# State-space heads of a two-layer diffusion backbone: one exponential and a predicated copy per head instead of masks and eight exponentials

## The reference

```python
seg = cum[:, :, :, None] - cum[:, :, None]
lmat = jnp.exp(jnp.where(causal, seg, -jnp.inf))
cb = jnp.einsum('bctgn,bcsgn->bctsg', cc, bc)
y_diag = jnp.einsum('bctsgh,bcsghp->bctghp', cb[..., None] * lmat, xdt)
...
y = (y_f + y_b + d_skip[:, None] * xs).reshape(bsz, m, SSM_D_INNER) * jax.nn.silu(z)
```

## Time and profile before

| | us |
|---|---|
| median of 3 runs | 2121.7 |
| lowest and highest | 2121.1, 2123.09 |
| the profiled execution's own time | 2116.36 |
| its span in the profile | 2114.6 |
| TensorE busy | 2039.2 |
| VectorE busy | 1275.2 |
| ScalarE busy | 863.0 |
| GpSimd busy | 114.3 |

### The profile page before, as it was taken

How to read it: one execution, slowest core, us unless ns; L and a number is a source line. 1 busy time by engine, 2 the same in 40 slices (tenths; PEclk the granted TensorE clock), 3 DMA queues, 4 the chain that set the end, 5 groups by cost and what they waited for, 6 DMA issues and landing times.

```text
span 2114.6 us, 33441 instructions
## 1 busy us (share of the span) xinstructions
PE 2039.2 (96%) x12674; PEld 1802.4 (85%) x12674; DVE 1275.2 (60%) x1958; ACT 863.0 (41%) x1392; POOL 114.3 (5%) x175
## 2 busy tenths in 40 slices
PE   6999999999999999999999999999998999999998
PEld 4899999998889999999998877778775787888887
DVE  7655655557475773764766767777777644333335
ACT  4544433434232341332433555748384325222222
POOL 1111001010010000000000100000000000000000
PEclk9999999999999999999999999999999999999999
DMA  8422232323422432433322221221216223333332
GB/s 311 140 81 83 68 90 81 91 61 120 119 87 78 138 116 80 138 96 96 98 88 66 77 70 41 66 64 50 89 48 230 64 86 86 93 99 97 93 99 90
DMA packets 297916, 204.68 MB, mean 97 GB/s; under 512 B 5396, under 2 KB 289421, under 8 KB 296013
## 3 DMA queue, kind: packets, MB, share of 16 engines
q1 hardware_dynamic: 294349, 180.04, 29.0%
q0 software_dynamic: 3456, 23.09, 3.0%
HBM read 189.47 MB, written 13.63 MB: 96 GB/s over the span
## 4 chain that ended last, share of the span: by engine, by line
PE 81%; DVE 8%; ACT 5%; issue 3%; DMA 1%; SPq 1%; ACTq 0%; POOL 0%; DVEq 0%; POOLq 0%
PE G L328 56%; PE G L1241 13%; ACT e L1995 1%; PE S L2133 1%; PE S L874 1%; DVE acc L2164 1%; PE S L2129 1%; PE S L845 1%; PE S L453 1%; DVE wlo L315 1%; DVE hlo L755 1%; DVE hn L746 1%; ACT whi L311 1%; PE G L437 1%; DMA ada<-in_ada_w_dram 1%
## 5 line engine op out<-in xcount | busy, mean ns | idle before, releaser
L328 PE MATMUL G<-hhi,whi 128*128 128x384 f32 (+2 forms) x1760 | 573.9, 377 | 25.5 <-DVE hlo L755 16.2
L315 DVE TENSOR_TENSOR wlo<-raw,whi 128x1024 fp32r<-128x1024 f32 (+2 forms) x213 | 248.0, 1165 | 471.9 <-ACT whi L311 471.3
L328 PE MATMUL G<-hhi,wlo 128*128 128x384 f32 (+2 forms) x1760 | 531.4, 352 | 0.0
L328 PE MATMUL G<-hlo,whi 128*128 128x384 f32 (+2 forms) x1760 | 531.0, 352 | 0.0
L311 ACT ACTIVATE whi<-raw 128x1024 fp32r<-128x1024 f32 (+2 forms) x213 | 215.9, 1014 | 718.6 <-PE G L328 584.5
L328 PEld LDWEIGHTS G<-hhi,whi 128*128 128x128 f32 x1760 | 318.8, 190 | 92.0 <-issue 39.6
L328 PEld LDWEIGHTS G<-hhi,wlo 128*128 128x128 f32 x1760 | 326.5, 190 | 20.1
L328 PEld LDWEIGHTS G<-hlo,whi 128*128 128x128 f32 x1760 | 327.1, 190 | 17.7
L328 PE MATMUL G<-mhi,whi 128*128 128x384 f32 (+2 forms) x544 | 163.6, 349 | 2.0 <-issue 0.9
L328 PE MATMUL G<-mhi,wlo 128*128 128x384 f32 (+2 forms) x544 | 162.6, 347 | 0.0
L328 PE MATMUL G<-mlo,whi 128*128 128x384 f32 (+2 forms) x544 | 162.5, 347 | 0.0
(11 more groups left out here) (356 smaller groups left out, 2991.6 us busy)
## 6 DMA issues: line engine op xcount, KB each, us to landing
raw<-in_ffn_w_in_dram SPq DMA_DIRECT2D x52, 512.0 KB, 4.0
raw<-in_ssm_w_in_dram SPq DMA_DIRECT2D x41, 512.0 KB, 4.0
raw<-in_hg_w_in_dram SPq DMA_DIRECT2D x40, 512.0 KB, 4.1
adaw<-in_ada_w_dram SPq DMA_DIRECT2D x20, 1024.0 KB, 5.3
adaf<-in_ada_w_dram SPq DMA_DIRECT2D x20, 1024.0 KB, 5.3
sraw<-in_ffn_w_in_dram SPq DMA_DIRECT2D x36, 512.0 KB, 5.1
raw<-in_ffn_w_out_dram SPq DMA_DIRECT2D x32, 384.0 KB, 3.6
raw<-in_ssm_w_out_dram SPq DMA_DIRECT2D x16, 512.0 KB, 4.1
```

What stands on the lines that cost most here:

```text
L315: dve.tensor_tensor(wlo[pn.slot][:, 0:kt, :], raw[pn.slot][:, 0:kt, :], f32(whi[pn.slot][:, 0:kt, :]), ALU.subtract).then_inc(s["lo"], 1)
L328: ins = pe.matmul(G[:, tl.slot, g0:g0 + n], w[pn.slot][:, k, :], r[:, k_base + k, t0:t0 + n], start=(first and k == 0 and i == 0), stop=(l ...
```

## The change

Per head TensorE issues one matmul for each direction. The selector `hsel` now has 48 rows, and `hrow` beside it holds the cuts of this group, so that the product already contains the shift that was ScalarE's bias. The masks are gone. The earlier direction is in bank 0, the later one in bank 1 for even and bank 3 for odd heads. ScalarE copies bank 0 to the tile `e` (`head_start`), VectorE overwrites the later direction's half from the other bank with a predicated copy under the constant mask `later` (`head_select`), and ScalarE takes one exponential of 128x512 in place (`head_decays`). VectorE multiplies by `cb`. Every output goes to bank 2, so that `heads_y` of hh waits for `head_out` of hh - 1.

A predicated copy gives each pair of tokens one direction, so a token's product with itself is counted once. The other one and the skip are computed on GpSimd (`own_tokens`) and added to `ytm` ahead of the heads' outputs, and `yb` is written by one multiplication with z. GpSimd also fetches the rows of each group from DRAM (`head_rows`).

```diff
-            def pair_decays(hh):
-                r = hh % 2
+            def head_start(hh):
                 act.wait_ge(s["sm"], HPG * q + hh + 1)
                 if hh >= 2:
                     act.wait_ge(s["yd"], HPG * q + hh - 1)
-                for d in (0, 1):
-                    for b in range(LBLK):
-                        ins = act.activation(block(m[f"e{d}{r}"][:, :], b), block(S[:, d, :], b), ACT.Exp,
-                                             bias=m["shiftT"][:, b, bass.ds(q * HPG + (d * NH + hh), 1)])
-                ins.then_inc(s["em"], 1)
+                act.activation(m[f"e{hh % 2}"][:, :], S[:, 0, :], ACT.Copy).then_inc(s["ec"], 1)
+            def head_decays(hh):
+                act.wait_ge(s["sl"], HPG * q + hh + 1)
+                e = m[f"e{hh % 2}"][:, :]
+                act.activation(e, e, ACT.Exp).then_inc(s["em"], 1)
...
                         if q is not None and 3 <= j < 7:
-                            pair_decays(2 * (j - 3))
-                        if q is not None and ci == 1:
-                            act.wait_ge(s["skip"], q * GT + GT)
+                            head_start(2 * (j - 3))
                         if ci:
                             convolved(ci - 1)
+                        if q is not None and 3 <= j < 7:
+                            head_decays(2 * (j - 3))
...
-                if q is not None and j == 1:
-                    act.wait_ge(s["yout"], q * 32 + 16)
-                    for i_ in range(GT):
-                        act.activation(m["yb"][:, i_, :], m["xfm"][:, i_, 0:NLAT], ACT.Identity,
-                                       scale=m["dsk"][:, bass.ds(q * GT + i_, 1)]).then_inc(s["skip"], 1)
                 if q is not None and 3 <= j < 7:
                     if before is None:
-                        pair_decays(2 * (j - 3))
-                    pair_decays(2 * (j - 3) + 1)
+                        head_start(2 * (j - 3))
+                        head_decays(2 * (j - 3))
+                    head_start(2 * (j - 3) + 1)
+                    head_decays(2 * (j - 3) + 1)
...
+        def later_bank(hh):
+            return 3 if hh % 2 else 1
+        def head_select(dve, q, hh):
+            dve.wait_ge(s["ec"], HPG * q + hh + 1)
+            dve.memset(m["carry"][:, :], 0.0)
+            dve.copy_predicated(by_block(m[f"e{hh % 2}"][:, :]), m["later"][:, :, :].to_broadcast([P, LBLK, P]),
+                                by_block(S[:, later_bank(hh), :])).then_inc(s["sl"], 1)
         def head_weights(dve, q, hh):
-            r = hh % 2
             dve.wait_ge(s["em"], HPG * q + hh + 1)
-            e0, e1 = m[f"e0{r}"][:, :], m[f"e1{r}"][:, :]
-            dve.tensor_tensor(e0, e0, e1, ALU.add).then_inc(s["mm"], 1)
-            dve.wait_ge(s["mm"], 2 * (HPG * q + hh) + 1)
-            dve.tensor_tensor(e0, e0, m["cb"][:, :], ALU.mult).then_inc(s["mm"], 1)
+            e = m[f"e{hh % 2}"][:, :]
+            dve.tensor_tensor(e, e, m["cb"][:, :], ALU.mult).then_inc(s["mm"], 1)
         def head_out(dve, q, hh):
+            if hh == 0:
+                dve.wait_ge(s["owna"], 2 * q + 2)
             dve.wait_ge(s["yd"], HPG * q + hh + 1)
             yt = m["ytm"][:, :, hh * HP:(hh + 1) * HP]
-            dve.tensor_tensor(yt, yt, S[:, 2 + hh % 2, 0:LBLK * HP].rearrange("p (b c) -> p b c", c=HP),
+            dve.tensor_tensor(yt, yt, S[:, 2, 0:LBLK * HP].rearrange("p (b c) -> p b c", c=HP),
                               ALU.add).then_inc(s["ym2"], 1)
...
+                h0 = 2 * (j - 3)
                 if q is not None and 3 <= j < 7:
-                    head_weights(dve, q, 2 * (j - 3))
                     if j > 3:
-                        head_out(dve, q, 2 * (j - 3) - 1)
+                        head_out(dve, q, h0 - 2)
+                    head_select(dve, q, h0)
+                    head_weights(dve, q, h0)
+                    if j > 3:
+                        head_out(dve, q, h0 - 1)
                 for u in range(4):
                     if q is not None and j < 3:
                         chain_vector(dve, q, 4 * j + u)
+                    if q is not None and 3 <= j < 7 and u == 3:
+                        head_select(dve, q, h0 + 1)
                     tap(u + 1)
                 if q is None:
                     for _ in range(DT_DVE.count(j)):
                         next(dt)
                 if q is not None and 3 <= j < 7:
-                    head_weights(dve, q, 2 * (j - 3) + 1)
-                    head_out(dve, q, 2 * (j - 3))
+                    head_weights(dve, q, h0 + 1)
                 if q is not None and j == 7:
                     if ss is None:
                         split_lo(dve, At(PAN_SO + SO_SPLITS[j]), KT)
+                    head_out(dve, q, HPG - 2)
                     head_out(dve, q, HPG - 1)
                     for i_ in range(GT):
                         yb = m["yb"][:, i_, :]
                         dve.wait_ge(s["ytt"], GT * q + i_ + 1)
-                        dve.tensor_tensor(yb, yb, S[:, i_, :], ALU.add).then_inc(s["ya"], 1)
-                    for i_ in range(GT):
-                        yb = m["yb"][:, i_, :]
-                        dve.wait_ge(s["ya"], GT * q + i_ + 1)
-                        dve.tensor_tensor(yb, yb, m["z"][:, bass.ds(q % 2, 1), i_, :].rearrange("p a t -> p (a t)"),
+                        dve.tensor_tensor(yb, S[:, i_, :], m["z"][:, bass.ds(q % 2, 1), i_, :].rearrange("p a t -> p (a t)"),
                                           ALU.mult).then_inc(s["yz"], 1)
...
+        def head_rows(pool, g):
+            hs = slice(g * HPG, (g + 1) * HPG)
+            for e in (0, 1):
+                for d in (0, 1):
+                    r = (2 * e + d) * HPG
+                    pool.dma_start(m["hrow"][r:r + HPG, :], cut_park[e, d, hs, :]).then_inc(s["hin"], 16)
+                    pool.dma_start(m["hsel"][HK + e * LBLK:HK + (e + 1) * LBLK, d * HPG:(d + 1) * HPG, :],
+                                   shift_park[e, d, hs, :].rearrange("h (b t) -> b h t", t=P)).then_inc(s["hin"], 16)
+        def own_tokens(pool, q):
+            def step(n, ins):
+                ins.then_inc(s["owns"], 1)
+                pool.wait_ge(s["owns"], 11 * q + n)
+            def heads(ap):
+                return ap.rearrange("p (b a) -> p b a", a=1).to_broadcast([P, LBLK, HPG])
+            pool.wait_ge(s["stc"], 6 * q + 2)
+            step(1, pool.tensor_tensor(by_block(m["own"][:, 0:NLAT]), by_block(m["cb"][:, :]),
+                                       ident[:, :].rearrange("p (a t) -> p a t", a=1).to_broadcast([P, LBLK, P]), ALU.mult))
+            half = P // 2
+            for n in range(7):
+                own = by_block(m["own"][:, 0:NLAT])
+                to = m["owncb"][:, 0:LBLK].rearrange("p (b a) -> p b a", a=1) if half == 1 else own[:, :, 0:half]
+                step(2 + n, pool.tensor_tensor(to, own[:, :, 0:half], own[:, :, half:2 * half], ALU.add))
+                half //= 2
+            step(9, pool.tensor_tensor(m["ownx"][:, :, :], m["dtT"][:, :, q * HPG:(q + 1) * HPG], heads(m["owncb"][:, 0:LBLK]),
+                                       ALU.mult))
+            step(10, pool.tensor_tensor(m["ownx"][:, :, :], m["ownx"][:, :, :],
+                                       m["dall"][:, q * HPG:(q + 1) * HPG].rearrange("p (a h) -> p a h", a=1)
+                                       .to_broadcast([P, LBLK, HPG]), ALU.add))
+            pool.wait_ge(s["stc"], 6 * q + 6)
+            pool.wait_ge(s["yout"], q * 32 + 16)
+            step(11, pool.tensor_tensor(m["xown"][:, :, :].rearrange("p b (h c) -> p (b h) c", c=HP),
+                                       m["xtm"][:, 0:LBLK, :].rearrange("p b (h c) -> p (b h) c", c=HP),
+                                       m["ownx"][:, :, :].rearrange("p b (h a) -> p (b h) a", a=1)
+                                       .to_broadcast([P, LBLK * HPG, HP]), ALU.mult))
+            pool.wait_ge(s["ymc"], 12 * q + 12)
+            for bs in (slice(0, 2), slice(2, 4)):
+                pool.tensor_tensor(m["ytm"][:, bs, :], m["ytm"][:, bs, :], m["xown"][:, bs, :], ALU.add)\
+                    .then_inc(s["owna"], 1)
...
-                pe.wait_ge(s["cbs"], q + 1)
+                pe.wait_ge(s["hcon"], 2)
+                pe.wait_ge(s["hin"], 128 * q + 128)
             else:
-                pe.wait_ge(s["em"], HPG * q + hh)
+                pe.wait_ge(s["ec"], HPG * q + hh)
+                if hh == 1:
+                    pe.wait_ge(s["ymc"], 12 * q + 12)
+                else:
+                    pe.wait_ge(s["sl"], HPG * q + hh - 1)
             for d in (0, 1):
-                pe.matmul(S[:, d, :], m["sel"][:, d * HPG + hh:d * HPG + hh + 1].to_broadcast([P, P]),
-                          m["cuts"][:, :], start=True, stop=False)
-                ins = pe.matmul(S[:, d, :], m["identb"][:, :], m[f"neg{d}"][:, :], start=False, stop=True)
```

(32 more changed lines are left out.)

61 lines of the change are left out of this document (34 added, 27 removed).

## The result

The changed kernel takes 2140.54 us (median of 5, 2139.38 to 2142.21) against 2121.85 (5 runs): ratio 1.0091, interval 1.0079 to 1.0102, so 18.7 us slower. The prediction said 2124, from 2113 to 2132.

The account below looks back on a forecast made before the run. TensorE, busy 2039.2 of 2114.6 us, was taken to bound the kernel. Loop +3.0, last group -7.3, GpSimd +3.1, layer start +2.3, small things +1.0 made +2.1 on 2121.7: 2123.8, stated as 2124, range 2113 to 2132.

Parts of the forecast that it names:

- It runs in panels 1 and 2: GpSimd's 2048-column product, 4.5 us, beside busy VectorE: 0.5 in the loop's first pass, 0 in the other two.
- +3.1: GpSimd's cost to VectorE: 0.5 in the loop, 1.5 in the last group's chain, 1.1 at its head 0; bounds 0, 14.
- Two matmuls instead of four: about 0.47.: One head's exponents on TensorE: 0.47 instead of 0.93 us, 0.46 saved, 14.7 us of work over 32 heads.
- The clock falls in the new waits (13%).: Rival, 13%: the clock falls at the outputs' waits of 2 to 3 us in the loop; three falls, +5.1, 2129.
- The price per fall, 1.7: Time lost per clock fall, 1.7 us, from 4.0 us at granted clock 0.57 behind the earlier kernel's last-group waits.
- The ring: ScalarE and VectorE alternate in a loop panel of 768 tokens: 11.75 us against 10.8; outputs wait 9.0 per group.
- +1.0 per group: Net cost in each of three loop groups: +2.3 up to head 7, less 1.3 recovered; +3.0 in all.
- taken as recovered: 1.3 us per loop group back behind head 7, since VectorE no longer adds the skip and its sums come earlier.
- The last group: TensorE binds the heads at 2.73 us instead of 3.45, and waits shrink: -7.3.
- The start of the layer: VectorE's first low split queues behind GpSimd's selector constant, so TensorE starts 2.3 us later: +2.3, bounds 0 and 3.6.
- The rival on the slow side: Rival, 20%: GpSimd's 2048-column product holds VectorE beyond TensorE's lead in every group, decided from about 4.7 us: 2131.

Follow-up runs that it names:

- 128 rows: Changed kernel with selector and rows zero-padded to 128 rows, so the exponents' matmuls read 128 rows: 2139.33 us, ratio 1.0080; also used in combined runs.
- the fill: Changed kernel with 24 matmuls of 128 columns, results unread, ahead of the last group's first output: 2139.26 us, ratio 1.0079.
- the triple: Changed kernel with GpSimd's additions moved to VectorE, outputs in two banks (later direction always bank 1), and 128 rows in the exponents' matmuls: 2120.09 us, ratio 0.9985.

## Why the prediction was wrong

*"It runs in panels 1 and 2 [...] I price it at 0.5 in the first pass of the loop and 0 in the other two."* This is the step that failed most. GpSimd was given +3.1, worked out from 4.5 us of one 2048-column operation in panels 1 and 2; 1.1 of it stands at the last group's head 0 with no operation named. The two additions of 1024 columns, counted just before, got neither a length nor a place. They take 2.78 each, start when the chain ends, and meet the tap and the split ahead of the first head. Leaving them out is worth 12.4 us. The product itself took 4.0, near the 4.5 of the prediction, and cost nothing that shows in the loop, but 3.0 in the last group's chain, where 1.5 was forecast.

*"Two matmuls instead of four: about 0.47."* This term failed too. The pair cost 0.66, and 0.1 at its neighbour; the saving per head was under 0.2, not 0.46. With 128 rows the pair takes the 0.45 that was predicted. In the loop this mattered little, since 128 rows gave nothing back there; in the last group, with the clock up in both, 128 rows are worth 1.0 us (26.0 and 25.0 with two banks and the additions moved).

*"The clock falls in the new waits (13%)."* It was a rival, and what it describes came about beside the rest. Windows of 2 us from 1240 to 1740 give 5.8 us lost to the clock before and 17.1 after. Of the 12.4 us, 7.2 lie in the last group's heads: 2 of them the longer wait, 5 behind it, which fits the 5.3 of the fill. The price per fall, 1.7, holds in two of the loop's groups (in the third it was 3.4); in the last group, where TensorE is busy throughout behind its first wait, it was 7 (14 us at half).

*The ring.* The mechanism was right: the loop's low splits at panels of 768 tokens lie 12.2 us apart where 11.75 was forecast, and TensorE waits for additions at heads 1, 3, 4, 5 and 7. The waits were 6.3 in the first group, not 9.0. Yet the sum of +1.0 per group missed by 3 to 4. In the first group the prediction's own terms, with what they measured, nearly make it up: 6.3 of waits, less 3.0 of old waits, less 1.3 saved on exponents, plus 1.7 lost to the clock is 3.7, an estimate, against 4.1 measured. The 1.3 "taken as recovered" behind the heads did not come: from a group's last output to the next group's first exponents it is 66.6 us before and after. Why the second and third group lost 5.0 stays open in part. That the additions' bank and the select bind together, so that lifting one gives a third, was not in the prediction at all.

*The last group.* -7.3 forecast (6.5 of it up to the last output, 22.6 us from 29.1), +6.1 measured. It came to 28.0 without GpSimd's additions and to 25.0 in the triple.

*The start of the layer.* +2.3 forecast. The first split takes 1.75 us instead of 1.22 and TensorE waits 0.5 longer, and the first exponents come 1.3 sooner after the layer's start than before:

```profile
1186.18 0.61 PE L333 MATMUL G<-hhi,whi 128*128 128x384 f32 x2 [1.00 <-DVE wlo L320]
```

The rival on the slow side had the right engine and the wrong operation: its condition, a product of 4.7 us or more, did not come true, and its 2131 was 10 short.
